# A hybrid attention and expert layer on one core: the first attention's softmax moved among the second's q and k groups, its half of the output projection behind the softplus, running sums in fp32r, and finer waits

## What is computed

```
xn = RMSNorm(h);  [q_m,k_m,v_m | q_s,k_s,v_s] = xn @ W_in
group M (8 heads): causal softmax attention, q and k RMS-normalised, relative bias
group S (8 heads): stick-breaking attention:
  z = q k^T / 8;  w = exp(log_sigmoid(z) + sum over s<j<t of log_sigmoid(-z_j))
h = h + concat(rms(o_m), rms(o_s)) @ W_out
h = h + PEER(RMSNorm(h))      128 x 128 experts, product keys, top 16 of 8 heads
h = h + sigmoid(RMSNorm(h) @ W_g) * (p @ W_ple)
```

## Time and profile before

| | us |
|---|---|
| median of 3 runs (lowest, highest) | 974.1 (973.94, 974.22) |
| the profiled execution's own time | 974.06 |
| its span, first to last instruction | 972.3 |
| TensorE busy | 959.7 |
| VectorE, ScalarE, GpSimd busy | 682.0, 607.6, 330.8 |

### The profile page before, as it was taken

How to read it: one execution, slowest core, us unless ns; L and a number is a source line. 1 busy time by engine, 2 the same in 40 slices (tenths; PEclk the granted TensorE clock), 3 DMA queues, 4 the chain that set the end, 5 groups by cost and what they waited for, 6 DMA issues and landing times.

```text
span 972.3 us, 19170 instructions
## 1 busy us (share of the span) xinstructions
PE 959.7 (99%) x6222; PEld 873.3 (90%) x6222; DVE 682.0 (70%) x1386; ACT 607.6 (62%) x1032; POOL 330.8 (34%) x148
## 2 busy tenths in 40 slices
PE   8999999999999999999999999999999999999998
PEld 5987889999999999999999999888888888888877
DVE  6747663999975888888888884555555555566663
ACT  7576664256666888888888885554554555555643
POOL 0002130178888777777777774000000000000000
PEclk9999999999999999999999999999999999999999
DMA  9772423044555444444444445555566766555521
GB/s 331 264 284 87 187 90 131 1 153 176 190 174 181 165 158 166 160 164 157 166 160 164 156 168 174 196 193 194 194 224 239 246 234 235 190 194 191 191 105 44
DMA packets 46603, 172.08 MB, mean 177 GB/s; under 512 B 5187, under 2 KB 8684, under 8 KB 45036
## 3 DMA queue, kind: packets, MB, share of 16 engines
q1 hardware_dynamic: 46284, 171.40, 50.2%
q10 hardware_dynamic: 288, 0.28, 0.1%
HBM read 169.55 MB, written 2.11 MB: 177 GB/s over the span
## 4 chain that ended last, share of the span: by engine, by line
PE 92%; DVE 3%; issue 2%; DMA 1%; SPq 1%; POOL 1%; ACT 1%; POOLq 0%; DVEq 0%
PE bank L1191 14%; PE bank L1192 14%; PE bank L1193 14%; PE pair L1502 12%; PE pair L1505 12%; PE pair L1504 12%; PE pair L1463 3%; PE pair L1219 1%; PE pair L1220 1%; PE pair L1221 1%; DMA w_raw<-w_in 1%; PE bank L1221 1%; PE bank L1219 1%; PE bank L1220 1%; PE bank L1545 1%
## 5 line engine op out<-in xcount | busy, mean ns | idle before, releaser
L573 ACT ACTIVATE t_hi<-t_raw 128x1024 fp32r<-128x1024 f32 x256 | 270.4, 1057 | 164.5 <-DMA t_raw<-v_chunks 161.2
L1163 POOL TENSOR_TENSOR t_lo<-t_raw,t_hi 128x1024 fp32r<-128x1024 f32 x130 | 312.2, 2415 | 151.9 <-ACT t_hi L573 151.9
L1191 PE MATMUL bank<-xt_hi,t_hi 128*128 128x256 f32 x1024 | 290.1, 283 | 0.1
L1192 PE MATMUL bank<-xt_lo,t_hi 128*128 128x256 f32 x1024 | 289.8, 283 | 0.0
L1193 PE MATMUL bank<-xt_hi,t_lo 128*128 128x256 f32 x1024 | 289.8, 283 | 0.0
L895 DVE TENSOR_TENSOR t_lo<-t_raw,t_hi 128x1024 fp32r<-128x1024 f32 x126 | 154.4, 1225 | 136.1 <-ACT t_hi L573 135.8
L1502 PE MATMUL pair<-t_hi,g_hi 128*128 128x512 f32 x512 | 199.4, 389 | 0.0
L1504 PE MATMUL pair<-t_lo,g_hi 128*128 128x512 f32 x512 | 199.2, 389 | 0.0
L1505 PE MATMUL pair<-t_hi,g_lo 128*128 128x512 f32 x512 | 199.2, 389 | 0.0
L1191 PEld LDWEIGHTS bank<-xt_hi,t_hi 128*128 128x128 f32 x1024 | 196.6, 192 | 0.3 <-POOL t_lo L1163 0.3
L1192 PEld LDWEIGHTS bank<-xt_lo,t_hi 128*128 128x128 f32 x1024 | 196.6, 192 | 0.0
(11 more groups left out here) (255 smaller groups left out, 1283.6 us busy)
## 6 DMA issues: line engine op xcount, KB each, us to landing
t_raw<-u_chunks SPq DMA_DIRECT2D x128, 512.0 KB, 3.2
t_raw<-v_chunks SPq DMA_DIRECT2D x128, 512.0 KB, 3.3
w_raw<-w_query SPq DMA_DIRECT2D x4, 2048.0 KB, 8.2
w_raw<-w_in SPq DMA_DIRECT2D x3, 2048.0 KB, 10.5
w_raw<-w_out SPq DMA_DIRECT2D x2, 2048.0 KB, 7.6
wg_raw<-w_gate SPq DMA_DIRECT2D x8, 512.0 KB, 4.4
w_raw<-w_in SPq DMA_DIRECT2D x7, 512.0 KB, 8.4
w_raw<-w_in SPq DMA_DIRECT2D x2, 1024.0 KB, 10.5
```

Source lines behind the costliest of these rows:

```text
L573: nc.scalar.activation(t_hi[:, q % RING, :], t_raw[:, q % RING, :], ACT.Copy).then_inc(t_hi_ready, 1)
L1163: nc.gpsimd.tensor_tensor(t_lo[:, q, :], t_raw[:, q, :], t_hi[:, q, :].bitcast(f32), ALU.subtract).then_inc(t_lo_pool, 1)
L1191: mm(dst, ah, bh, start=(c == 0), stop=False)
L1192: mm(dst, ah, bl, start=False, stop=False)
```

## The change

`w_in` is reordered: group 2 is now v of M, 3 and 4 are q and k of S. The softmax of M stands between quarters of groups 3 and 4. Its output is transposed to tiles of its own (`ot_hi`, `ot_lo`), split by VectorE, and three of its four pieces of the output projection run while ScalarE does the softplus of S; its norm comes from `Ln` and `Exp` in place of `Sqrt`. The softplus is split into two fp32r parts (`sp_hi` by ScalarE, `sp_lo` by VectorE), and each running sum is ten fp32r matmuls in place of five in fp32. The second half of the output weights (group 7) is split in two pieces by both engines (`second_out_hi`, `second_out_lo`). TensorE waits for the k group of M by quarters and for v of M by halves, and at the end for pairs of transposed columns in place of fours. The two first embeddings go ahead of the second norm's transposes, the two others between them.

```diff
-Q_M, K_M, Q_S, K_S, V_M, V_S = range(6)
+Q_M, K_M, V_M, Q_S, K_S, V_S = range(6)
...
+        ot_hi = tile("ot_hi", [P, 4, SEQ], ZONE + 4 * 11264, f32r)
+        ot_lo = tile("ot_lo", [P, 4, SEQ], ZONE + 4 * 12288, f32r)
+        sp_hi = tile("sp_hi", [P, 2, 1536], ZONE + 4 * 8192, f32r)
+        sp_lo = tile("sp_lo", [P, 2, 1536], ZONE + 4 * 5120, f32r)
+        tri_r = tile("tri_r", [P, 2, P], ZONE + 4 * 4096, f32r)
...
+            if part == 0:
+                return 6 + tt if g == 0 else (6, 3)[tt]
+            return (4 if g == 0 else 2) + tt
...
+            return (out_done, 6 + 2 * (n - OUT0)) if n < QUERY0 else (w_used, n + 1 - (QUERY0 - OUT0))
...
+            nc.scalar.preload_act_table(ACT.Exp)
+            split_group(4)
...
+            act.wait_ge(s_shifted, 1)
+            nc.scalar.activation(s0[:, :, :], s0[:, :, :], ACT.Exp).then_inc(s_exp, 1)
             split_group(5)
+            for k in range(2):
+                act.wait_ge(s_shifted, 2 + k)
+                nc.scalar.activation(s1[:, 4 * k:4 * k + 4, :], s1[:, 4 * k:4 * k + 4, :], ACT.Exp).then_inc(s_exp, 1)
+            for b in range(6):
+                weights_out(b)
+            split_group(6)
+            for tt in range(TT):
+                act.wait_ge(pv_out, tt + 1)
+                squares(1, tt, tt, o_nat[:, tt, 0:512], s0[:, 4 * tt:4 * tt + 4, :].rearrange("p a b -> p (a b)"))
 
...
-            nc.scalar.preload_act_table(ACT.Exp)
-            split_group(6)
-            split_group(7)
+            _, ms, r_out = norm_stats(1)
+            act.wait_ge(mean_ready, 3)
+            nc.scalar.activation(ms[:, 0:2], ms[:, 0:2], ACT.Ln).then_inc(first_log, 1)
+            act.wait_ge(first_log, 1)
+            nc.scalar.activation(r_out[:, 0:2], ms[:, 0:2], ACT.Exp, scale=-0.5).then_inc(first_rstd, 1)
+
+            def second_out_hi(k):
+                if k == 0:
+                    act.wait_ge(w_loaded[1], 16 * 3)
+                    act.wait_ge(*used(V_S))
+                c = slice(4 * k, 4 * (k + 1))
+                nc.scalar.activation(w_hi[:, 1, c, :], w_raw[:, 1, c, :], ACT.Copy).then_inc(w7_hi_ready, 1)
+
+            second_out_hi(0)
+            for e in range(2):
+                act.wait_ge(sp_masked, e + 1)
+                nc.scalar.activation(sp_hi[:, e, :], sb_sp[:, e, :], ACT.Copy).then_inc(sp_split_hi, 1)
+            second_out_hi(1)
             for e in range(2):
                 act.wait_ge(cum_done, e + 1)
...
+            nc.scalar.preload_act_table(ACT.Sqrt)
...
+            for tt in range(TT):
+                act.wait_ge(ot_done, 3 + tt)
+                for c in range(4):
+                    ins = nc.scalar.activation(xt_hi[:, 4 + c, P * tt:P * (tt + 1)], ot_half(1, tt, c), ACT.Copy,
+                                               scale=gain[:, 1, 4 + c:5 + c])
+                ins.then_inc(ot_hi_ready, 1)
+            act.wait_ge(spv_out, 2)
+            for tt in range(TT):
+                squares(1, 2 + tt, tt, o_nat[:, tt, 512:1024], xs[:, tt, 512:1024])
+            act.wait_ge(mean_ready, 4)
...
+            split_group(3)
...
+            biased(0, s0, 0, 4, P)
+            biased(1, s1, 0, 2, 0)
+            biased(2, s1, 4, 2, 0)
+            shifted(0, s0[:, :, :], MX0, P)
+            shifted(1, s1[:, 0:4, :], MX1[:, 0:4], SEQ)
+            dve.wait_ge(row_ready, 1)
+            columns_scaled(Q_S)
+            shifted(2, s1[:, 4:8, :], MX1[:, 4:8], SEQ)
+            softmax_sum(0, s0)
+            split_group(5)
+            attended(0)
+            softmax_sum(1, s1)
+            columns_scaled(K_S)
+            attended(1)
+
...
+            first_split(0)
+            first_split(1)
+            mean(1, 4, 0, 2, 512)
+            split_group(6)
+            nc.vector.tensor_copy(tri_r[:, :, :], cst[:, 1:3, :]).then_inc(tri_ready, 1)
+            value_out(1, 0)
...
+            def second_out_lo(k):
+                c = slice(4 * k, 4 * (k + 1))
+                dve.wait_ge(w7_hi_ready, k + 1)
+                nc.vector.tensor_tensor(w_lo[:, 1, c, :], w_raw[:, 1, c, :], w_hi[:, 1, c, :].bitcast(f32),
+                                        ALU.subtract).then_inc(w7_lo_ready, 1)
...
+            softplus_added(0)
+            value_out(1, 1)
+            softplus_added(1)
+            dve.wait_ge(first_rstd, 1)
+            projected(0, 0, 0)
+            second_out_lo(0)
+            softplus_lo(0)
+            projected(0, 1, 0)
+            softplus_lo(1)
+            projected(1, 0, 0)
+            second_out_lo(1)
+            for tt in range(TT):
+                t = slice(P * tt, P * (tt + 1))
+                dve.wait_ge(ot_hi_ready, 3 + tt)
+                for c in range(4):
+                    ins = nc.vector.scalar_tensor_tensor(out=xt_lo[:, 4 + c, t], in0=ot_half(1, tt, c),
+                                                         scalar=gain[:, 1, 4 + c:5 + c],
+                                                         in1=xt_hi[:, 4 + c, t].bitcast(f32), op0=ALU.mult,
+                                                         op1=ALU.subtract)
+                ins.then_inc(ot_lo_ready, 1)
+            projected(1, 1, 0)
+            mean(1, 6, 2, 4, 512)
+            link(inverse(1, 3, 2, 4))
...
-            dve.wait_ge(*used(OUT0))
-            for tt in range(TT):
-                for part in range(2):
-                    projected(0, tt, part)
+            for tt in range(TT):
+                projected(0, tt, 1)
             dve.wait_ge(w8_hi_ready, 1)
             nc.vector.tensor_tensor(w_lo[:, 0, 0:4, :], w_raw[:, 0, 0:4, :], w_hi[:, 0, 0:4, :].bitcast(f32),
                                     ALU.subtract).then_inc(w8_lo_ready, 1)
-            for part in range(2):
-                projected(1, 0, part)
+            projected(1, 0, 1)
             norm2_scaled(0)
-            projected(1, 1, 0)
             projected(1, 1, 1)
             norm2_scaled(1)
...
+                    for c in range(DC):
+                        if n == K_M and tt == 0 and c % 2 == 0:
+                            pe.wait_ge(quarter_lo, DC + c // 2 + 1)
+                        if n == V_M and tt == 0 and c % 4 == 0:
+                            pe.wait_ge(half_lo, c // 4 + 1)
+                        mm(bank[b + tt][:, :], xt_hi[:, c, t], w_hi[:, n % 2, c, :], start=(c == 0), stop=False)
+                        mm(bank[b + tt][:, :], xt_hi[:, c, t], w_lo[:, n % 2, c, :], start=False, stop=False)
+                        ins = mm(bank[b + tt][:, :], xt_lo[:, c, t], w_hi[:, n % 2, c, :], start=False,
+                                 stop=(c == DC - 1))
                     if tile_done and tt == 0:
...
-            pe.wait_ge(group_out, 2)
-            columns_group(Q_S, 4)
+            rows_group(V_M, 4, v_tile_done, ready=((group_out, 1), (group_out, 2)))
+            pe.wait_ge(group_out, 4)
+            columns_group(Q_S, 6, (0,))
...
+            pe.wait_ge(qk_biased, 3)
+            columns_group(K_S, 4, (0,))
+
+            pe.wait_ge(s_exp, 1)
+            for hh in range(NH):
+                ins = nc.tensor.transpose(bank[hh // 4][:, P * (hh % 4):P * (hh % 4 + 1)], s0[:, hh, :], ident)
+                if hh % 4 == 3:
+                    ins.then_inc(pt_done, 1)
+            columns_group(K_S, 4, (1,))
+            pe.wait_ge(pt_out, 2)
+            pe.wait_ge(columns_out, 2)
+            for hh in range(NH):
...
+            pe.wait_ge(pv_out, 2)
+            out_transposes(0, 1)
+            rows_group(V_S, 6, v_tile_done, ready=((ot_lo_ready, 1), (ot_lo_ready, 2)))
...
             def running_sum(e):
-                pe.wait_ge(sp_masked, e + 1)
-                lower, upper = sb_sp[:, e, 0:1024], sb_sp[:, e, 1024:1536]
-                for b in range(2):
-                    mm(bank[3 * e + b][:, :], neg_tri, lower[:, 512 * b:512 * (b + 1)], start=False, stop=False,
-                       skip_group_check=True)
-                    mm(bank[3 * e + b][:, :].rearrange("p (i t) -> p i t", i=2)[:, :, P:SEQ], neg_ones,
-                       upper[:, 256 * b:256 * (b + 1)].rearrange("p (i t) -> p i t", i=2), start=False, stop=True,
-                       skip_group_check=True)
-                mm(bank[3 * e + 2][:, :], neg_tri, upper, start=False, stop=True,
-                   skip_group_check=True).then_inc(cum_done, 1)
-
+                tri, ones = tri_r[:, 0, :], tri_r[:, 1, :]
+                pe.wait_ge(sp_split_lo, e + 1)
+                for k, half_of in ((0, sp_hi), (1, sp_lo)):
+                    lower, upper = half_of[:, e, 0:1024], half_of[:, e, 1024:1536]
+                    for b in range(2):
+                        mm(bank[3 * e + b][:, :], tri, lower[:, 512 * b:512 * (b + 1)], start=False, stop=False,
+                           skip_group_check=True)
+                        mm(bank[3 * e + b][:, :].rearrange("p (i t) -> p i t", i=2)[:, :, P:SEQ], ones,
```

(79 more changed lines are left out.)

321 lines of the change are left out of this document (139 added, 182 removed).

## The result

| | time, us (runs) | ratio to before, 95% interval |
|---|---|---|
| before | 974.15 (973.93 to 974.45, 6) | |
| changed | 979.94 (975.95 to 982.09, 6) | 1.005 (1.0036 to 1.0065) |

The change makes the kernel 0.5% slower; the forecast was 976.3 within 971.7 to 978.8. The direction was right and the size too small by 3.6 us. One thing was not foreseen at all: the six runs of the changed kernel lie 6 us apart, those of before 0.5. The profiled execution took 981.81, span 980.1, where before had 972.3: 7.8 more.

The account below looks back on a forecast made before the run. TensorE bounds the kernel, busy 959.7 of 972.3 us, so only its own work and waits count. Costs of 12.1 less gains of 10.0, 2.2 unrounded, added to 974.06 gave 976.3, range 971.7 to 978.8.

Parts of the forecast that it names:

- (1): Second output group: TensorE waits 3.1 for `w_lo` ahead of `projection(1, 0, 0)`, plus 0.35 for `v_out`; bounds 2.2, 4.0.
- (2): Masks of w: TensorE waits 1.9 for GpSimd's mask ahead of the first `sb_w` matmul; bounds 1.0 and 2.5.
- (a): TensorE's earlier waits at group 1, attention, projection and second norm go: 6.0 gained, including group 1's 1.5.
- (c): The end: with pairs of columns ScalarE starts after two transposes; the 0.7 wait with its overlap goes, 0.8 gained.
- (b): Running sums: fp32r matmuls in place of fp32 take both sums from 6.9 to 3.7, a gain of 3.2.
- (3): Tail, second norm: GpSimd's subtractions and VectorE exclude each other; TensorE waits 2.05 for `wp_lo` and 2.5 for `xs`.
- (4): First query group: embeddings no longer cover the high and low parts after the transposes; cost 1.95, bounds 1.0 and 2.4.
- (5): M part between quarters of groups 3 and 4: first softmax copies 0.25 late; bounds 0 and 2.
- The stop does not bite: Rival: GpSimd, VectorE run together; 2.05 and 2.5 go, mask's 0.5, 0.5 of (1); less 4.6: 971.7 or less; chance 0.14.
- only two-input operations are stopped: Rival, tail: the scaling slips through, but tile 1's addition is held; query start 2.4 earlier, 974.0; chance 0.18.
- More is late: Rival: the one-column mean is stopped too (0.8), and (1)'s 16.8 or a load comes 1 to 2 later; 978.3; chance 0.20.

## Why the prediction was wrong, and where it was right

**The step that failed** is the sum of the costs. It put each pause of TensorE at its own length, (1) at 3.1 and (2) at 1.9, and what a pause does to the work behind it at nothing, without a reason: it stands in no term and in no rival. The runs showed that behind these pauses the granted clock can halve. That was 6.6 us in the profiled execution and 4.7 in the median (by so much the median falls with both pauses filled), and putting a pause of 3.1 into the kernel before cost 8.0 beyond the pause. The 1.9 of (2) was right as a wait and wrong as a price, because 48 matmuls stand behind it that then took 9.98 instead of 5.57. Without the clock the forecast stands 1.0 above the median with both pauses filled (975.3) and 1.7 above the 974.6 worked out from the runs' clocks. The profile of before held a hint that I did not read: its clock is 1.00 throughout, but in that stretch its longest wait is 0.9. The change made waits longer than any there, so the 1.00 was not given.

**(a), (c), the waits of before.** Group 1 and the end: 2.45 forecast, 2.55 measured alone. Right. The other waits of before that the change removes were not measured by themselves.

**(b), the running sums.** The fp32r matmuls of 512 and of 256 columns started 0.23 and 0.12 apart, as forecast; the 3.2 are right as work. Their worth is 1.9, because the rest was cover for the masks; the prediction booked the same fact as part of cost (2).

**How the costs are measured.** The prediction counts a wait from the true end of the matmul before it, the list of waits from the modelled end some 0.15 later. What follows counts as the prediction did, from starts, with the list's figure in brackets.

**(1) `w_lo` of the second output group.** 2.0 (1.86) instead of 3.1, and for `v_out` 0.3 instead of 0.35: the second projection piece starts at 96.53, just behind `v_all`'s end at 96.47. ScalarE's chain from z took 16.6 (16.8 forecast), with the loads at 1.28 each:

```profile
91.24 1.28 ACT L506 ACT_TABLE_LOAD   x1
92.54 2.86 ACT L506 ACTIVATE sb_sp<-sb_sp 128x1536 f32<-128x1536 f32 x2
...
95.51 1.28 ACT L511 ACT_TABLE_LOAD   x1
```

In this trace 91.24 + 1.28 is 92.52, and Ln starts at 92.54. The further 1.38 of drain that the Trainium skill (ScalarE: Activation LUTs, What ACT_TABLE_LOAD costs) gives is not there either. VectorE, forecast 0.9 late, was 0.0 late: its additions and subtractions got in ahead of GpSimd's masks instead of behind them, and the masks paid (5.97 for four, where two took 1.23 before, with ScalarE waiting 1.71 for them). The exclusion was right, its order wrong.

**(2), the masks of w.** 1.9 (1.73) against 1.9; see above for what follows it.

**(3), the tail.** `wp_lo` was 7.07 long with VectorE's 2.31 in between, and TensorE waited 1.5 (1.37) against 2.05. The scaling was stopped until GpSimd's end, and TensorE waited 2.3 (2.15) against 2.5. The mechanism was right, and is shown by taking the collision away.

**(4), the first query.** From the second tile's transposes at 146.67 to the end of the first quarter at 152.52 are 5.85 against 5.8 forecast: a cost of 2.0 against 1.95. Only 1.2 of it stands in the list of waits. **(5), the softmax copies.** 0.9 (0.7) instead of 0.25.

**The sum.** In all, the listed costs came to 10.9 instead of 12.1. Less the 10.0 forecast as gained, that is 0.9 later; with both pauses filled the median is 1.0 later. The largest miss among them is (1), 1.1 too high; the schedule as a whole was read well, and the clock came on top.

**The rivals.** "The stop does not bite" and "only two-input operations are stopped" are refuted by 4.40 beside 0.76, though the 0.15 and 0.17 of the small operations show that "VectorE's SBUF-to-SBUF work stands still" was too wide. If the two halves of a microsecond that the first of them names beside its 4.6 are meant to go too, its time is 970.7 and not 971.7. "More is late" came 1.6 short of the measured time, and for another reason.

## What to carry to other kernels

Here a pause of TensorE had two prices, its own length and that of the work behind it at half clock. Before a change opens a wait, look at what follows it, and price that work at both clocks: here 48 matmuls took 9.98 us instead of 5.57, and more stood behind them. If the wait can't go, put real work into it, or even idle work. A spread between runs that grows while the schedule doesn't is a reason to look at the granted clock first. Subtractions on GpSimd belong where VectorE has no long operation from SBUF to SBUF to do: order them by waits, not by chance.

## What the runs showed that was not expected

- A pause of 1.7 to 1.9 us was followed by a fall of 10 to 14 us where matmuls of 64 columns came next, and by one of 3.4 where 512 columns came next; one of 3.1 gave 17 us, and a mean clock as low in each of the four runs. What sets the length of a fall stays open: no run changed the work behind a pause and nothing else. And not each pause does it. In the changed kernel's profiled execution the first (1.86) did not, nor did those of 1.4 and 2.2 at 137 and 141, nor the 1.9 in group 0. With the first pause filled, the 2.1 at 141 was followed by 0.50 from 142.5 to 145.9. In the kernel before, 1.5 ahead of group 1 was followed by 1.00.
- A fall can also stand at the very start: in the run with GpSimd held back the clock was 0.50 from 8.4 to 11.8 us, behind the wait in group 0 that all these kernels share (2.0 there).
- A mean clock a little under 1 says nothing certain of one run's time. Of the runs of the kernel before that were taken beside the experiments, the 11 with 0.998 have a median of 974.9, the 5 with 0.997 one of 973.9, and the 37 with 1.000 one of 974.1. No trace of a run of it with a lowered clock was taken.
- Queued behind a running GpSimd operation, VectorE's operation got in when GpSimd changed from one instruction to the next: the 128 x 1 addition at 136.86 ended 0.06 after the change at 137.74, and the next GpSimd subtraction was not delayed by it (4.55).
